# Key and query columns of a latent attention packed into fewer weight tiles

## The reference, cut to what matters

```
q = (rmsnorm(c_q, q_a_norm) @ w_uq).reshape(B, S, 8, 64 + 32)        # c_q: 384 wide
kv = (rmsnorm(c_kv, kv_a_norm) @ w_ukv).reshape(B, S, 8, 64 + 64)    # c_kv: 256 wide
k = concatenate([kv[..., :64], broadcast(k_pe, 8 heads)], -1)        # k_pe: 32 wide, one for all heads
q, k = rmsnorm(q, q_norm), rmsnorm(k, k_norm)                        # over the 96 columns of a head
q, k = [q[:64], rope(q[64:])], [k[:64], rope(k[64:])]                # rotates 16 columns against 16
o = block_causal_attention(q, k, v)
```

## Time and profile before

| | |
|---|---|
| time, median of 3 runs | 2617.48 us (2617.39 to 2620.05) |
| time of the profiled execution | 2617.04 us |
| span of the profiled execution | 2615.3 us |
| PE busy | 2595.3 us, 99% |
| DVE / ACT / POOL busy | 1373.6 / 971.9 / 151.4 us |
| stages `ei` to `ev` | from 1265.6 to 1400.1 us of the span |

### The profile page before, as it was taken

The page is one execution under the profiler, slowest core; times in us unless marked ns, Lnnn a source line. Parts: engine busy times, 40 slices in busy tenths (PEclk is TensorE's granted clock), DMA queues, the critical chain, the costliest instruction groups (busy, mean ns, idle before and its releaser), DMA issues.

```text
span 2615.3 us, 30767 instructions
## 1 busy us (share of the span) xinstructions
PE 2595.3 (99%) x12322; PEld 2118.6 (81%) x12322; DVE 1373.6 (53%) x2142; ACT 971.9 (37%) x1531; POOL 151.4 (6%) x169
## 2 busy tenths in 40 slices
PE   9999999999999999999999999999999999999999
PEld 8867888888888788888876888888888688888887
DVE  4375773664435776376577544344542365544343
ACT  4274442343226643244447432233222233432231
POOL 0230000000001100000040000000110400000000
PEclk9999999999999999999999999999999999999999
DMA  4311223232231133223221233223232022233222
GB/s 159 130 58 65 93 87 103 97 108 101 98 103 60 41 102 108 89 97 105 94 73 45 83 102 105 89 97 104 90 129 81 17 99 95 97 97 105 96 97 82
DMA packets 66799, 240.50 MB, mean 92 GB/s; under 512 B 7712, under 2 KB 7840, under 8 KB 66528
## 3 DMA queue, kind: packets, MB, share of 16 engines
q1 hardware_dynamic: 63936, 229.38, 26.4%
q0 software_dynamic: 2720, 9.15, 1.1%
HBM read 236.37 MB, written 2.13 MB: 91 GB/s over the span
## 4 chain that ended last, share of the span: by engine, by line
PE 94%; ACT 3%; DVE 2%; issue 1%; POOL 0%; DMA 0%; SPq 0%; DVEq 0%; POOLq 0%; ACTq 0%
PE ps L452 30%; PE ps L454 30%; PE ps L453 30%; PE ps L861 1%; PE ps L565 1%; ACT m_A_P L1767 1%; ACT m_B_P L1767 1%; PE ps L848 1%; PE ps L580 1%; PE ps L600 0%; DVE m_A_P L1025 0%; PE ps L760 0%; ACT m_E_P L1767 0%; PE ps L517 0%; DVE m_A_P L1063 0%
## 5 line engine op out<-in xcount | busy, mean ns | idle before, releaser
L452 PE MATMUL ps<-m_xs,m_wsp 128*128 128x512 f32 x2232 | 874.6, 392 | 1.5 <-DVE m_xs L933 1.5
L453 PE MATMUL ps<-m_xs,m_wsp 128*128 128x512 f32 x2232 | 869.0, 389 | 0.0
L454 PE MATMUL ps<-m_xs,m_wsp 128*128 128x512 f32 x2232 | 869.0, 389 | 0.0
L1658 ACT ACTIVATE m_wsp<-m_raw 128x1024 fp32r<-128x1024 f32 (+1 forms) x429 | 446.0, 1051 | 779.0 <-PE ps L454 745.4
L906 DVE TENSOR_TENSOR m_wsp<-m_raw,m_wsp 128x1024 fp32r<-128x1024 f32 (+1 forms) x429 | 518.5, 1225 | 153.2 <-ACT m_wsp L1658 153.1
L452 PEld LDWEIGHTS ps<-m_xs,m_wsp 128*128 128x128 f32 x2232 | 419.3, 188 | 93.0 <-issue 7.1
L454 PEld LDWEIGHTS ps<-m_xs,m_wsp 128*128 128x128 f32 x2232 | 419.3, 188 | 87.8
L453 PEld LDWEIGHTS ps<-m_xs,m_wsp 128*128 128x128 f32 x2232 | 419.5, 188 | 87.6 <-issue 1.7
L959 DVE TENSOR_TENSOR m_x<-m_x,ps 128x512 f32<-128x512 f32 x104 | 71.1, 687 | 317.9 <-PE ps L454 317.9
L452 PE MATMUL ps<-m_wsp,m_xs 128*128 128x512 f32 x320 | 126.6, 396 | 0.0
L454 PE MATMUL ps<-m_wsp,m_xs 128*128 128x512 f32 x320 | 125.2, 391 | 0.0
(11 more groups left out here) (303 smaller groups left out, 3198.0 us busy)
## 6 DMA issues: line engine op xcount, KB each, us to landing
m_raw<-in_w SPq DMA_DIRECT2D x427, 512.0 KB, 3.3
m_A_cb<-csum POOLq DMA_DIRECT2D x16, 256.0 KB, 4.1
m_x<-in_xT SPq DMA_DIRECT2D x4, 512.0 KB, 6.8
m_B_bias<-in_biasB POOLq DMA_DIRECT2D x8, 256.0 KB, 3.1
out<-m_x SPq DMA_DIRECT2D x8, 256.0 KB, 2.0
m_raw<-in_w SPq DMA_DIRECT2D x4, 256.0 KB, 5.9
m_O_D<-in_decay POOLq DMA_DIRECT2D x1, 1024.0 KB, 5.0
m_O_cs<-in_ropeo POOLq DMA_DIRECT2D x1, 512.0 KB, 4.9
```

The lines of the kernel that those rows point to most:

```text
L452: e.matmul(out, lh, rh, start=first, stop=False)
L453: e.matmul(out, lh, rl, start=False, stop=False)
L454: return e.matmul(out, ll, rh, start=False, stop=final)
L1658: e.activation(wsp[n % NSP][:, 0, o:1024], raw[n % NRAW][:, o:1024], ACT.Copy).then_inc(*s_hi(n))
```

## The change

- Weights: `ei` has five groups, key latents first, and no tile for the shared key. `ek` has four outputs of two heads each. `eq` has six: first the rotary columns of all heads (16 first halves, then 16 second halves of each of eight heads), then four of two heads' plain columns. A stage may end inside a chunk; the rest of it stays empty (`eq`: 18 of 24 tiles).
- The shared key is made in a hook at tile 20 of `ei` by eight float32 matmuls on `x` itself in four strips, with 32 weight columns that POOL loads and scales. DVE evacuates four strips and adds them; two DMAs swap the halves.
- Squares are kept for two heads side by side. Sums go to four strips, head `h` to strip `h % 4`; the shared key's squares and the rotary queries' squares are added by strips of their own. The hooks lie at other tiles.
- DVE evacuates two halves of a bank into two heads (`ek`, `eq`), and rotates all heads' queries at once with six instructions on 128x512. POOL spreads the result over the heads by sixteen DMAs. A `group_norm` follows each pair.
- The reciprocal for queries moves from `ei` to `eg`, and the `x_final` instructions are spread otherwise.

```diff
-    add("ei", "ei", 8, [[0, 1]] + singles(2, 6))
-    add("ek", "ukv", 2, singles(0, 8))
-    add("eg", "ei", 8, [range(10, 14)])
-    add("eq", "uq", 3, singles(0, 8))
-    add("eu", "ei", 8, singles(6, 10))
-    add("ev", "ukv", 2, [range(8, 12)])
+    add("ei", "ei", 8, [[3, 4]] + singles(0, 3))
+    add("ek", "ukv", 2, singles(0, 4))
+    add("eg", "ei", 8, [range(9, 13)])
+    add("eq", "uq", 3, [[4], [5]] + singles(0, 4))
+    add("eu", "ei", 8, singles(5, 9))
+    add("ev", "ukv", 2, [range(4, 8)])
...
+            def shared_key():
+                b = take("main", "kp")
+                q.wait_ge(*free[b])
+                q.wait_ge(*s_wkp["wkp"])
+                for k in range(8):
+                    q.wait_ge(*s_x["f1.dn1", k])
+                    j = k % 4
+                    i = e.matmul(ps[b][32 * j:32 * j + 32, :], E_wkp[:, 32 * k:32 * k + 32], x[:, k, :], start=k < 4,
+                                 stop=k >= 4, skip_group_check=True)
+                i.then_inc(*s_kp("kp"))
+                free[b] = s_step["kp", 3]
...
+            hooks = {8: [xstat("fm"), xstat("m2_0")], 15: [row("m2_0")], 20: [shared_key], 22: [row("fm")],
+                     26: [xstat("kva", 2)], 36: [row("kva")]}
...
+            def head_sums(kind, pairs):
+                for p in pairs:
+                    q.wait_ge(*s_sq["e" + kind, p])
+                for p in pairs:
+                    of = E_sq[(p if kind == "k" else p + 1) % 2]
+                    for j in range(2):
+                        h = 2 * p + j
+                        i = strip(kind, h % 4, E_oneh[0:64, h // 4, :], of[0:64, j, :], kind == "k" and p < 2,
+                                  kind == "q" and p >= 2)
+                return i
...
+            def key_sums(*pairs):
 
                 def hook():
+                    if pairs[0] == 0:
+                        new_sums("k")
+                    i = head_sums("k", pairs)
+                    if pairs[-1] == 3:
+                        q.wait_ge(*s_sq["kpe"])
+                        for j in range(4):
+                            i = strip("k", j, E_oneh[64:96, 6, :], E_rt[1][64:96, :], False, True)
+                    i.then_inc(*s_sums(*(("k", p) for p in pairs)))
+                return hook
+            def query_sums(*pairs):
+                def hook():
+                    if pairs[0] == 0:
+                        new_sums("q")
+                        q.wait_ge(*s_rope["squares"])
+                        for j in range(4):
+                            strip("q", j, E_oneh[:, 2 + j, :], E_sq[0][:, 0, :], True, False)
+                    i = head_sums("q", pairs)
...
 ...
-                    {8: [row("kva")]})
+                    {5: [xstat("qa", 3)]})
             project_rows(ST["eg"], xhalf, lambda k: s_xlo["fm", k], lambda ci, tb: s_aev["eg", ci, tb],
-                         hooks={4: [pair_sums("k", 0), pair_sums("k", 1)], 8: [pair_sums("k", 2)], 12: [pair_sums("k", 3)],
-                                16: [columns("k")], 20: [key_scale(0), key_scale(1)], 24: [key_scale(2), key_scale(3)],
-                                28: [key_scale(4), key_scale(5)]})
...
             project(ST["eu"], xhalf, lambda k: s_xlo["fm", k], lambda m: s_ev["eu", m],
-                    {2: [pair_sums("q", 1)], 8: [pair_sums("q", 2)], 12: [pair_sums("q", 3)], 16: [gate(0)],
-                     18: [columns("q")], 20: [gate(1)], 24: [gate(2)], 28: [gate(3)]})
+                    {2: [query_sums(0)], 12: [query_sums(1, 2)], 16: [gate(0)], 18: [query_sums(3)], 20: [gate(1)],
+                     24: [columns("q"), gate(2)], 28: [gate(3)]})
...
+            def shared_key():
+                parts = (E_kpe[64:96, :], E_rt[0][64:96, :], E_rt[1][64:96, :], E_sq[0][64:96, 0, :])
+                q.wait_ge(*s_kp["kp"])
+                q.wait_ge(*s_rowc["m2_0"])
+                for j, t in enumerate(parts):
+                    r = slice(32 * j, 32 * j + 32)
+                    e.tensor_tensor(t, bank("kp")[r, :], R[r, :], ALU.mult).then_inc(*s_step(("kp", j)))
+                q.wait_ge(*s_step["kp", 1])
+                e.tensor_tensor(parts[0], parts[0], parts[1], ALU.add).then_inc(*s_step(("kp", 4)))
+                q.wait_ge(*s_step["kp", 3])
+                e.tensor_tensor(parts[2], parts[2], parts[3], ALU.add).then_inc(*s_step(("kp", 5)))
+                q.wait_ge(*s_step["kp", 5])
+                e.tensor_tensor(parts[0], parts[0], parts[2], ALU.add).then_inc(*s_step(("kp", 6)))
...
+                    if m in (1, 2, 4):
+                        add_square(*latent(m))
+                    if m == 0:
+                        shared_key()
+                    if m == 1:
                         factors("kva")
+                    if m == 2:
+                        shared_key_turned()
...
+                if m >= 4:
+                    if m == 5:
+                        q.wait_ge(*s_sums["k", 3])
+                    e.tensor_tensor(E_rt[m - 4][:, :], bank("eq", m)[:, :], E_rb[0][:, :], ALU.mult).then_inc(*s_ev(("eq", m)))
+                    if m == 5:
+                        query_rope()
+                    return
+                e.tensor_tensor(E_q[0:64, 2 * m, :], bank("eq", m)[0:64, :], E_rb[0][0:64, :], ALU.mult)
+                e.tensor_tensor(E_q[0:64, 2 * m + 1, :], bank("eq", m)[64:128, :], E_rb[0][64:128, :],
+                                ALU.mult).then_inc(*s_ev(("eq", m)))
+                group_norm(m)
+            def query_rope():
...
+                turned(o1, x1, "gqa", E_cos).then_inc(*s_step(("qrope", 0)))
+                turned(o2, x2, "gqb", E_sin).then_inc(*s_step(("qrope", 1)))
+                q.wait_ge(*s_step["qrope", 1])
+                e.tensor_tensor(o1[:, :], o1[:, :], o2[:, :], ALU.subtract).then_inc(*s_step(("qrope", 2)))
+                q.wait_ge(*s_step["qrope", 2])
+                turned(o2, x2, "gqb", E_cos).then_inc(*s_step(("qrope", 3)))
+                q.wait_ge(*s_sq["eq", 4])
+                turned(x1, x1, "gqa", E_sin).then_inc(*s_step(("qrope", 4)))
+                q.wait_ge(*s_step["qrope", 4])
+                e.tensor_tensor(o2[:, :], o2[:, :], x1[:, :], ALU.add).then_inc(*s_step(("qrope", 5)))
...
+                 {0: [lambda: factors("qa"), finals(0, 1)], 1: [finals(2, 3, 4), key_factors],
+                  2: [lambda: key_scaled(0), lambda: key_scaled(1), finals(5, 6, 7), lambda: key_scaled(2), lambda: key_scaled(3)],
+                  3: [lambda: key_scaled(4), lambda: key_scaled(5), lambda: key_scaled(6), lambda: key_scaled(7)]})
...
+                q.wait_ge(*s_ev["ek", m])
+                if m >= 2:
+                    q.wait_ge(*s_sums["k", m - 2])
+                e.activation(E_sq[m % 2][0:64, :, :], E_k[0:64, 2 * m:2 * m + 2, :], ACT.Square).then_inc(*s_sq(("ek", m)))
                 if m == 0:
+                    root("qa", 384)
...
+                q.wait_ge(*(s_sums["k", 3] if m in (0, 4, 5) else s_sums["q", max(0, m - 2)]))
+                if m >= 4:
+                    e.activation(E_sq[0][:, m - 4, :], E_rt[m - 4][:, :], ACT.Square).then_inc(*s_sq(("eq", m)))
+                else:
+                    e.activation(E_sq[(m + 1) % 2][0:64, :, :], E_q[0:64, 2 * m:2 * m + 2, :],
+                                 ACT.Square).then_inc(*s_sq(("eq", m)))
+                    tb = m
...
+            load(E_wkp, a["wkp"], d_wkp, "wkp")
             load(E_rope[:, :], a["ropem"], d_rope, "rope")
+            load(E_cos[:, :], a["ropeq"][:, 0, :], d_cos, "cos")
+            q.wait_ge(*d_wkp["wkp"])
+            q.wait_ge(*s_ones["gfm"])
+            w = E_wkp.rearrange("p (k c) -> p k c", k=8)
+            e.tensor_tensor(w, w, gfm[:, :].rearrange("p (k o) -> p k o", o=1).broadcast_to([128, 8, 32]),
+                            ALU.mult).then_inc(*s_wkp("wkp"))
+            q.wait_ge(*s_wkp["wkp"])
             q.wait_ge(*d_gmw["gmw"])
             e.memset(E_wt[64:128, :, 0:64], 0.0).then_inc(*s_zero("wt"))
             q.wait_ge(*s_zero["wt"])
+            q.wait_ge(*s_step["kp", 6])
+            load(E_kpe[96:112, :], E_kpe[80:96, :], d_swap, "first")
+            load(E_kpe[112:128, :], E_kpe[64:80, :], d_swap, "all")
+            q.wait_ge(*s_step["kpe", 2])
+            load(E_sin[:, :], a["ropeq"][:, 1, :], d_sin, "sin")
             for m in range(8):
-                q.wait_ge(*s_step["kpe", 2])
                 e.tensor_copy(E_k[64:96, m, :], E_kpe[64:96, :]).then_inc(*s_kpe(m))
+            q.wait_ge(*s_kpe[7])
+            q.wait_ge(*s_sq["eq", 5])
+            e.tensor_tensor(E_sq[0][:, 0, :], E_sq[0][:, 0, :], E_sq[0][:, 1, :], ALU.add).then_inc(*s_rope("squares"))
+            q.wait_ge(*s_step["qrope", 2])
+            for h in range(8):
+                load(E_q[64:80, h, :], sqs[0][16 * h:16 * h + 16, :], d_spread, ("first", h))
+            q.wait_ge(*s_step["qrope", 5])
+            for h in range(8):
```

(41 more changed lines are left out.)

208 lines of the change are left out of this document (90 added, 118 removed), and 2 rows, old and new, of the table _COLS.

## The result

The changed kernel takes 2638.76 us (median of 4 runs, 2637.46 to 2640.45), the kernel before 2617.96 beside it: ratio 1.0078 [1.0067, 1.009]. It is slower by 20.8 us. Forecast were 2611.6 with a range from 2605 to 2618; the time lies far outside, and on the side that had 7 in 100.

What follows compares the result with a forecast made beforehand. The tensor engine, busy 99% of the span, was taken to bound the kernel. Gains of 16.3 us less new waits of 10.9 gave -5.4 against the profiled 2617.04: 2611.6 us, range 2605 to 2618.

Steps and rivals of the forecast that it cites:

- I count 0.68 a tile: Price of a weight tile (three matmuls) on PE: 0.68 us; 22 tiles removed from `ei`, `ek`, `eq` give 15.0 us.
- the spread: Slower rival: sixteen loads spreading rotated queries run one behind the other and hold the scores, 2634 us; chance 0.06.
- rival 1: Four strips of the float32 sums run as two pairs: +5.2 us, 2616.8, no change; chance 0.13.
- the sums: Float32 sums of keys and queries on PE, in strips: 9.3 us before, 7.8 after, so -1.5.
- the two waits of before: PE waits that would go: 0.4 us before `row("kva")` and 1.2 before `columns("q")`.
- 16.3: PE's total gain in us before new waits: 14.7 without any wait, plus the two waits of before.
- (a): Transposes of `row("kva")`, at tile 36 of `ei`: PE waits 1.9 us for DVE, delayed by `shared_key`.
- (b): `ek` and the start of `eg`: fourth bank 0.3 us late, squares for `key_sums(0, 1)` another 0.8; wait 1.1.
- (c): Second chunk of `eu`: PE waits 6.8 us for DVE's `lo`, issued behind the group norms; bounds 4 and 9.
- (d): Behind (c) in `eu`: `gate(0)` waits 0.8 us after group norm 3, a `lo` costs 0.3; together 1.1.
- one of its own signs of being wrong: Prediction is wrong if PE waits over 2 us at a place not named.
- Rival 2: DVE isn't late in `eq`: without (c) and (d), 7.9 us less, 2603.7; chance 0.13.

Runs made afterwards that it cites:

- kernel with all edits: Changed kernel, `line` 16 columns; early low part, shared key before tile 0, banks moved, group norms one evacuation later, hooks moved: 2606.29 us, ratio 0.995 to the kernel before.
- the filled run: Changed kernel with `line` at 16 columns, plus 30 useless matmuls ahead of the `eu` tile that waits: 2622.49 us, ratio 1.0015 to the kernel before.

## Why the prediction was wrong

**The step that failed first** is one that priced nothing: "I count 0.68 a tile", for every stage, and only terms of `ei` to `ev` in the sum. The two new columns of `cf` are in the diff, and their only cost looked like 8 bytes of a load. They cost 15.6 us (2638.76 against 2623.18), three quarters of the slowdown: a product on a shifted tile takes 0.2333 us, not 0.227. No row of before could give the price; that tiles move could be read in the diff. No rival had it, and the one on the slower side (the spread) was about something else: the 16 loads landed 2.1 us after issue, and no scores waited.

**The gain was sized right.** The rounds of sums: shared key 1.86 us for 16 records (forecast 1.9), so four strips run at once and rival 1 is out; `ek` 6.48 (6.3); `eq` 12.64 (12.2, the rest `E_cs`'s start). Three terms came out smaller: the sums saved 1.2 us and not 1.5, the two waits of before were worth 1.3 and not 1.6, and the start of `E_cs` cost 0.5, together 1.1. In the kernel with all edits, waits of 0.5 in `ei` and 1.3 in `eg` were left; 16.3 less these 1.8 and 1.1 is 13.4, and the region up to `ev` is 13.4 shorter.

**The waits stood where they were put, and cost more.** The worst miss inside the region is that the sum counted waits and no clock. The idle time on a row is less than the whole cost, since a record ends later than the next could start, and since the products behind it can run at half clock. So the cost is counted here from start to start of the records in the kernel after, less what the same hook and products take without a wait.
- (a) Forecast 1.9; 3.9. The row has 2.5 of it; the clock is about 1.2.
- (b) Forecast 1.1; 1.3, with 0.5 and 0.3 on the rows at the named places. Right.
- (c) Forecast ready at T+26.5, wanted at T+19.8. It came at T+28.2 and was wanted at T+20.5: 7.8 for 6.8. A round of evacuation and norm took 4.9, not 4.7. Then 2.6 more, start to start, for the clock and the products behind it, of which the filled run gave back 2.2. Together 10.4.
- (d) Forecast 1.1; 1.3. From the gate to the next product it is 2.10 us instead of 0.82, with 0.65 and 0.13 idle on the rows.
- "DVE is as far as it was before" at the end of `eu` held, but the banks did not: the attention lasts 2.1 longer, with a wait of 2.4 at a place that the prediction did not name, which was one of its own signs of being wrong.

Together: 2.0 at (a), 0.2 at (b), 3.6 at (c), 0.2 at (d), 1.1 for the three smaller terms and 2.1 in the attention come to 9.2, which is what lies between -5.4 and +3.8. So `eq` starts 3.8 us earlier than before, counted from `ei`, and not 6.6. What stays open is how much of the attention's 2.1 the banks brought on.

Rival 2, no lateness of DVE, would have been right of the region in the kernel with all edits, for a reason that the prediction did not see: the order in which DVE's stops for ACT are taken, not its load. That the region is 13.25 shorter there and rival 2 says 13.3 is partly luck: it keeps 3.0 us of waits at (a) and (b), where that kernel had 1.8 and the 1.1 of the smaller terms.

## What to carry over

Before a tile is grown or added, list what lies behind it in a partition: a shift of 32 bytes costs every product whose two operands then no longer start at a multiple of 512 from each other (256 may do, but was not tried), here 3% on 2,496 of them. Price a new wait of the tensor engine with the half clock that follows it, 0.3 to 0.5 of the wait here; where it can't be avoided, useless products shortened the stage of one execution, though the medians don't show it. When work is taken from the bounding engine, the engine that feeds it must get its chains interleaved before it is called too slow: each norm set one evacuation later, with one low part ahead of the last, gave 6.9 us.

## What the runs showed of the hardware

Float32r products of 512 columns, weights loaded and features streamed, start 0.2267 us apart when the starts of the two operands are a multiple of 512 bytes apart, and 0.2289 to 0.2341 at the seven other differences of the table; a shift of everything together costs nothing (ratio 0.9996). A wait of 2.5 us of the tensor engine was followed by 3 us at a granted clock of 0.50, one of 7.8 us by over 4. Thirty matmuls whose results nobody reads, put into the longer wait, kept the clock at 1.00 and made the stage 2.2 us shorter in the profiled execution.
